# Eight heads in one pipeline: states and output of a head beside grams, inverse and attention of the next

## The reference, cut to what matters

```python
# A: sparse attention (the indexer's choice arrives as an additive mask)
logits = q @ k.T * 128 ** -0.5 - slope[h] * abs(t - s)      # masked
o_a = softmax(logits) @ v * silu(z_A)
# B: gated DeltaNet
qkv = silu(causal_conv(qkv_b, width 4));  q, k = l2norm(q), l2norm(k)
gc = cumsum(g);  decay = exp(gc[i] - gc[j]) where j <= i
M = I + strict_lower((beta * k) @ k.T * decay)
u, w = M^-1 @ (beta * v), M^-1 @ (beta * k * exp(gc))
for each chunk:                                   # here tiles of 128 tokens
    v_new = u - w @ S
    o = (q * exp(gc)) @ S + (q @ k.T * decay) @ v_new
    S = S * exp(gc_last) + (k * exp(gc_last - gc)).T @ v_new
o_b = rmsnorm(o) * silu(z_B)
y = x + concat(o_a, o_b) @ w_out;  final rmsnorm
```

## Time and profile before

| | us |
|---|---|
| three runs | 3327.34, 3342.03, 3343.69 |
| median | 3342.03 |
| span of the profiled execution | 3344.3 |

### The profile page before, as it was taken

One profiled execution on the slowest core, in us unless ns is written; L12 is line 12 of the kernel. 1 busy time (PEld: TensorE's weight loads), 2 busy tenths in 40 slices (PEclk: granted clock), 3 DMA queues, 4 the chain that ended last, 5 costly groups with the idle time before them and its releaser, 6 DMA issues. The chain is left out here.

```text
span 3344.3 us, 46103 instructions
## 1 busy us (share of the span) xinstructions
PE 2967.6 (89%) x16691; PEld 2657.3 (79%) x16691; DVE 1357.6 (41%) x2550; ACT 1025.5 (31%) x1995; POOL 887.9 (27%) x607
## 2 busy tenths in 40 slices
PE   4999899999999999999995588788878885799997
PEld 3999598998989899899995477667767774487876
DVE  6000101917463260705000667767776763214042
ACT  4111112213121211212112455565555553222221
POOL 6222021121212122121222223313422330155553
PEclk6999699999999999999997699999999997599998
DMA  3221222121212212122224111121121013346553
GB/s 129 62 65 60 43 69 73 49 72 49 67 57 64 62 60 73 56 66 63 69 64 133 36 49 50 41 69 34 35 69 48 27 41 88 125 155 208 175 180 120
DMA packets 271700, 255.47 MB, mean 76 GB/s; under 512 B 58712, under 2 KB 222752, under 8 KB 269152
## 3 DMA queue, kind: packets, MB, share of 16 engines
q1 hardware_dynamic: 261536, 208.80, 21.1%
q10 hardware_dynamic: 10048, 45.27, 3.3%
HBM read 190.48 MB, written 63.56 MB: 76 GB/s over the span
## 5 line engine op out<-in xcount | busy, mean ns | idle before, releaser
L394 PE MATMUL bank<-hH,wL 128*128 128x384 f32 (+1 forms) x2928 | 981.5, 335 | 14.9 <-POOL wL L311 14.9
L395 PE MATMUL bank<-hL,wH 128*128 128x384 f32 (+1 forms) x2928 | 980.1, 335 | 0.0
L396 PE MATMUL bank<-hH,wH 128*128 128x384 f32 (+1 forms) x2928 | 979.9, 335 | 0.0
L311 POOL TENSOR_TENSOR wL<-raw,wH 128x512 fp32r<-128x512 f32 x244 | 314.6, 1290 | 1388.7 <-ACT wH L328 1388.7
L394 PEld LDWEIGHTS bank<-hH,wL 128*128 128x128 f32 (+1 forms) x2928 | 550.1, 188 | 19.2 <-issue 18.5
L395 PEld LDWEIGHTS bank<-hL,wH 128*128 128x128 f32 (+1 forms) x2928 | 550.0, 188 | 0.8
L396 PEld LDWEIGHTS bank<-hH,wH 128*128 128x128 f32 (+1 forms) x2928 | 550.0, 188 | 0.7
L328 ACT ACTIVATE wH<-raw 128x512 fp32r<-128x512 f32 x244 | 154.2, 632 | 1019.3 <-PE bank L396 964.4
L1949 POOL TENSOR_TENSOR owL<-oraw,owH 128x2048 fp32r<-128x2048 f32 x48 | 225.5, 4700 | 271.4 <-ACT owH L1969 271.4
L506 DVE TENSOR_SCALAR score<-relued,w_idx 128x512 f32<-128x512 f32 (+3 forms) x10 | 7.8, 778 | 683.5 <-ACT relued L353 683.1
L1026 POOL TENSOR_TENSOR Bm<-A,keep_level 128x512 f32<-128x512 f32 x168 | 207.8, 1264 | 216.6 <-DVE A L1547 121.3
(11 more groups left out here) (297 smaller groups left out, 4028.8 us busy)
## 6 DMA issues: line engine op xcount, KB each, us to landing
raw<-in_w_in SPq DMA_DIRECT2D x240, 256.0 KB, 2.8
oraw<-in_w_out SPq DMA_DIRECT2D x48, 1024.0 KB, 5.0
proj_scratch<-ptbuf ACTq DMA_DIRECT2D x60, 576.0 KB, 2.8
xin<-proj_scratch SPq DMA_DIRECT2D x24, 512.0 KB, 4.8
mraw<-mix_scratch SPq DMA_DIRECT2D x12, 768.0 KB, 5.6
x<-in_x_prompt SPq DMA_DIRECT2D x8, 1024.0 KB, 5.0
out_y_prompt<-yv ACTq DMA_DIRECT2D x8, 1024.0 KB, 4.0
ox<-in_x_prompt SPq DMA_DIRECT2D x8, 768.0 KB, 6.6
```

The costliest lines, as they stand in the source:

```text
L311: pool.tensor_tensor(wL[c % 2][:, :, :], raw[c][:, :, :], wH[c % 2][:, :, :].bitcast(F32), ALU.subtract).then_inc(low_ready, 1)
L394: pe.matmul(o, low, hH[:, kk, tok], start=first, stop=False)
L395: pe.matmul(o, high, hL[:, kk, tok], start=False, stop=False)
L396: last = pe.matmul(o, high, hH[:, kk, tok], start=False, stop=end)
```

## The change

- All eight heads are written out; no loop is left in the stage. One list holds ten iterations, -2 to 7. Iteration i takes from head i the states (M), samples (S) and output (O), from head i+1 turns, grams, inverse and solves (D) and the attention (A), from head i+2 the convolution and its norms (N). Each step has a place between 0 and 1 in its iteration, and the list is sorted by it:

```diff
+def spread(first, last, steps):
+    return [(first + (last - first) * (i + 0.5) / len(steps), step) for i, step in enumerate(steps)]
+def iteration(i):
+    placed = []
+    if 0 <= i < H:
...
+        placed += spread(0.0, 0.36, states) + spread(0.36, 0.52, sample) + spread(0.52, 0.66, out)
...
+    if 0 <= i + 1 < H:
...
+        placed += spread(0.0, 0.07, turns) + spread(0.07, 0.26, grams) + spread(0.26, 0.30, first)
+        placed += spread(0.30, 0.93, levels) + spread(0.93, 1.0, solves)
...
+        placed += spread(0.0, 0.95, attend)
...
+    if 0 <= i + 2 < H:
...
+        placed += spread(0.05, 0.12, taps) + spread(0.12, 0.46, conv) + spread(0.46, 0.50, gates)
+        placed += spread(0.66, 0.90, natural) + spread(0.90, 1.0, norms)
...
+        placed += [(0.78, ("L_x", i + 3, 0))]
+    return [step for _, step in sorted(placed, key=lambda item: item[0])]
```

- PSUM: banks 0 and 1 serve states, samples, output and the turns of N in this order; banks 2 to 4 serve D; 5 and 6 the logits; 7 probabilities and values. The levels lag by one step, with two copies of WT, and both products of a step share a bank with its first one:

```diff
+        def w_bank(s):
+            return D_BANK + (0 if s == 0 else (2 * s - 1) % 3)
+        def z_bank(s):
+            return D_BANK + ((2 * s + 2) % 3 if s < NS - 1 else (2 * s + 1) % 3)
...
-                    if s >= LAG:
-                        r = s - LAG
+                    if s >= 1:
+                        r = s - 1
```

- Decays: mask and cumulated gates are summed in PSUM, for both triangles at once; ACT takes the exponential straight from there, the row's own gate as its bias. The grams are multiplied for two tiles at a time:

```diff
+                            pe.matmul(out, K["identb"][:, :], K["maskTN"][:, s, halves, :], start=True, stop=False)
+                            for part in range(2):
+                                last = pe.matmul(out, K["glog"][:, h, part, t:t + 1].to_broadcast([P, P]), K["cum2"][:, s, :, :], start=False, stop=part == 1)
...
+                        do(de[p % 2][:, t - lo, t_half, :], cum[:, t - lo, t_half, :], ACT.Exp, bias=K["gates"][:, h, G_NEG, t:t + 1])
+                        last = do(de[p % 2][:, t - lo, n_half, :], cum[:, t - lo, n_half, :], ACT.Exp, bias=K["gates"][:, h, G_POS, t:t + 1], scale=-1.0)
```

- Convolution: prompt and samples lie in one row per channel, the samples' old inputs between them as padding, so that a tap is one instruction over 1179 columns:

```diff
-                    V.scalar_tensor_tensor(out=y[:, n, 0:SEQ], in0=xin[:, n, j:j + SEQ], scalar=w, in1=y[:, n, 0:SEQ], op0=ALU.mult, op1=ALU.add).then_inc(convolved.sem, 1)
-                    ys = y[:, n, SEQ:].rearrange("p (b t) -> p b t", b=DEC_B)
-                    V.scalar_tensor_tensor(out=ys, in0=xsm[:, n, :, j:j + DEC_T], scalar=w, in1=ys, op0=ALU.mult, op1=ALU.add).then_inc(convolved.sem, 1)
+                    V.scalar_tensor_tensor(out=y[:, n, :], in0=xc[:, n, j:j + YC], scalar=K["cw"][:, n * H + h, 3 * DEC_B + j:3 * DEC_B + j + 1], in1=y[:, n, :], op0=ALU.mult, op1=ALU.add).then_inc(convolved.sem, 1)
```

- Attention: the distance term and the extreme value are one DVE instruction per part of at most 512 columns; the probabilities are scaled by their sum before they are turned, so that the product with v comes out turned, and the turn of the result is gone:

```diff
+                    V.tensor_tensor_reduce(out=lg[t % 2][:, c:e], in0=big[:, LG_BANK + i % 2, 0:e - c], in1=K["alibi"][:, at + c:at + e], scale=-SCALE, scalar=smallest,
+                                           op0=ALU.add, op1=ALU.min, accum_out=am[:, t, q // 4:q // 4 + 1]).then_inc(lg_ready.sem, 1)
...
+                    V.tensor_scalar(lg[t % 2][:, 0:w], lg[t % 2][:, 0:w], am[:, t, 3:4], None, ALU.mult).then_inc(p_scaled.sem, 1)
...
-                            last = pe.matmul(big[:, 7, 0:P], PT[t % 2][:, kb, :], K["vN"][:, kb, kv, :], start=(kb == 0), stop=(kb == t))
+                        last = pe.matmul(big[:, PV_BANK, 0:P], K["vN"][:, kb, h // GROUP, :], PT[t % 2][:, kb, :], start=(kb == 0), stop=(kb == t))
```

```diff
-                    if t >= 2:
+                    if t:
                         wait(pe, o_ready, h, t)
-                    pe.matmul(big[:, 2 + t % 2, 0:P], qkT[:, t, 0, :], S[:, :], start=True, stop=True)
+                    pe.matmul(big[:, 1, 0:P], qkT[:, q_slot(h), t, :], S[:, :], start=True, stop=True)
```

More of the change, by code:

```diff
@@ L710, in _ @@
                 dve.wait_ge(drained, NT)
[L711 to L761, removed]
-    s = LEVEL_STEPS.index((SAMPLE_LEVELS - 1, 4)) + LAG + 4
-    for step, every in (("D_solve_sample", 0), ("D_sample_state", 2), ("D_sample_turn", 3), ("D_sample_new", 1), ("D_sample_out", 2)):
-        s += every
-        levels.insert(levels.index(("D_level", s)), (step, 0))
-    order += levels
-    rest = ([] if last else [("N_done", 0)]) + score(4)
-    for t in range(4, NT):
-        rest += attend(t, t + 1 < NT)
-    rest += [("A_turn_o", NT - 1)]
-    if not last:
-        k = len(rest) * 3 // 4
-        rest = weave(rest[:k], NORMS[2:]) + rest[k:]
-    states = [("D_solve", 0)]
-    for t in range(NT):
-        states += [("D_read", t)] + ([("D_solve", t + 1)] if t + 1 < NT else []) + [("D_state", t), ("D_square", t - 1 if t else NT)]
-    return order + weave(states, rest) + [("D_square", NT - 1)]
@@ L793, in run_heads, with whole_order @@
+def whole_order():
+    order = [("L_x", 0, 0)]
+    for i in range(-2, H):
+        order += iteration(i)
+    return order
 def run_heads(nc, io, scratch, keep, ident):
@@ L1191, in _ @@
[L1191 to L1196 removed]
+                    wait(act, lg_ready, h, PARTS_TO[t])
@@ new lines, in values @@
+                def values(h, t):
+                    wait(pe, p_ready, h, PARTS_TO[t])
+                    for kb in range(t + 1):
+                        last = pe.matmul(big[:, PV_BANK, 0:P], K["vN"][:, kb, h // GROUP, :], PT[t % 2][:, kb, :], start=(kb == 0), stop=(kb == t))
+                    last.then_inc(pv_done.sem, 1)
+                run({"N_tails": tails, "N_turn": natural, "D_turn": qk_turn, "D_gram": gram, "D_first": first, "D_level": level, "D_solve": solve,
+                     "M_read": read, "M_state": state, "S_state": sample_state, "S_turn": sample_turn, "S_out": sample_out, "O_out": out,
+                     "A_logits": logits, "A_turn_p": turn_p, "A_values": values})
@@ L1540, in gram @@
[L1540 to L1547 removed]
+                    wait(dve, rooted, h, 1)
@@ L1629, in kept_tensors @@
+                run({"N_pads": pads, "N_conv": conv, "N_sum": sums, "N_norms": head_norms, "N_unit": unit, "D_gram": gram, "D_first": first, "D_level": level,
+                     "M_read": read, "M_state": state, "S_new": sample_new, "S_out": sample_out, "O_norm": out_norms, "O_out": out,
+                     "A_bias": bias, "A_norm": normalise, "A_gate": gate})
 def kept_tensors(nc, ctx):
```

1020 lines of the change are left out of this document (500 added, 520 removed).

## The result

The changed kernel takes 3302.91 us in the median of four runs (3300.03 to 3304.17), the kernel before 3342.86 beside it: ratio 0.9876, 95% interval 0.9851 to 0.9901. It is faster, by 40 us (1.2%); the forecast was 3212 us, 131 less. The direction held, the size did not: a third of the gain came.

A forecast was written before the change was run, and what follows sets the result against it. No engine was full, PE nearest; its 84.3 us of passes a head at 86% gave period P = 98. Ends and seven periods, 168 + 7P, replaced 986.6 us: T = 2525.7 + 7P = 3212 us, range 3135 to 3320.

The forecast's parts named there:

- P: Period of one head in the pipelined eight-head stage: 118.1 us before, forecast 98, with 92 to 104 as its range.
- Iteration -2: Start of the pipeline, the first head's convolution alone: 43 us (40 to 50) in place of 51.5.
- the tail: Last iteration, only the last head's states, samples and output: 38 us (30 to 48).
- the tables: Set-up ahead of the stage, 24 short transposes, two DMAs, small DVE steps: +2 us (0 to +5).
- 86%: Share of a full iteration that PE's 84.3 us of passes were taken to fill, giving a period of 98 us.
- The waits that I named: Norms to next head's first turn, SiLU block, inverse's first steps, state reading behind output sum: 2 to 4 us each, 14 in all.
- iteration 6 without convolution, P - 4: Second-last iteration, with no convolution left to do: 4 us shorter than a full one, 94 at P = 98.
- Iteration -1: Second iteration at the pipeline's start, without states: some 72 us of PE work, 88 us (75 to 105).
- Dense: Rival: three chains fill each other's gaps on PE as in the 96% stretch; P = 88, 3142 us; chance 0.15.
- One step of lag: Rival: PE waits 1.2 us for ACT's copy in each of 27 inverse steps; P = 126, 3408 us; chance 0.12.
- DVE held by POOL: Rival: port lock delays 20 DVE instructions 1.5 us each, DVE 98; P near 108, 3282 us; 0.20 with slower mixes.
- Nothing comes of it: Rival: waits of one order on in-order engines line heads up again; P 114 to 118, 3324 to 3352 us; chance 0.08.

## Why the prediction was wrong

**What held.** The range of 3135 to 3320 us holds the time, but not by the forecast's own mechanism: that ended at P = 104, and 112.65 falls under the 0.20 kept for "DVE held, and slower mixes up to P = 114". PE's work: 84.0 us priced, 84.3 forecast. DVE 70.2 a period (68), ACT 57.6 (59), POOL 32.1 (35.9), five table loads, PE's records 665 (a few under 675). Iteration -2 and the tail came 2 and 6 us under their terms; the tables cost 2.8 for 2. The loop's 3.0 us on issue are gone, but PE's first reading of a state stands 2.5 us on issue instead, because the state's clearing on DVE comes behind the two scalings of the norms.

**What failed** is one step: "I take 86%, midway between the 75% of the two large stages and 96%: 98 us." One density was put over three stages that have different limits. By stage, at 86%, the front would have taken 24.3 us, the levels 65.8, the end 7.6; they took 33.1, 67.3 and 12.2. So 8.8 and 4.6 of the 14.7 us lie in front and end, where the trace of before already had 51%, and where the change put two chains, but little of PE's other work: attention was spread by count of steps, and its first tiles are the small ones. In their place the runs show a front whose length hangs on the preparation of the next head, which stands in the same queues: 33.1 us as it is, 29.7 with most of the convolution's columns gone, 26.1 in iteration 6, which has none of that preparation. (The clock rises on the way, from 0.91 to 0.99 and 0.96, and no run parts its share.) The end is held by the norms: it takes 7.9 us with them moved ahead, though the levels pay that back. The run with four times the turns shows that PE's passes don't set the front's length there, the run with the largest tiles first that filling it pays.

**The waits that I named** were sized nearly right: first steps 4.2 us (3.07 and 1.14 in a row), SiLU block 2.3, reading for the output sum 2.3, norms 2.5, together 11.3 where 14 stood. They were not the whole: PE's gaps of over 0.15 us in the timeline sum to 18.6 us a period, and the remaining 10.0 (112.6 - 84.0 - 18.6) are passes that last longer than priced, alone or at 1.2 GHz. The granted clock of the three stages (0.91, 0.98, 0.81) makes 13 us of a period at the lower clock; at most half of that is lost. The prediction had no term for it in the period.

**A second mis-sized term**: iteration 6 without convolution, P - 4. It came out at 93.8 as forecast, but that is luck: P was 14.7 too small and the deduction 14.9, since the full iteration is 18.9 longer, not 4. Taking most of the columns from the multiply-adds gave 6.7 of that, clock included; the taps and SiLUs on ACT, the turns and the norms are the rest, which no run took apart. Iteration -1, with convolution and without states, took 99.0 where 88 stood: its front has some 15 us of passes in 28.9.

**The rivals.** *Dense* fell: only the levels came near. *One step of lag* fell: PE's second product waits 2.3 us a period for the copy, once, at the SiLU block, against 32 needed:

```profile
PE big L1280 <- ACT WT L1040: 2.3, 1, 2.3
```

*DVE held by POOL* would have given 108, near the result, by another way than what happened: the nine long convolution steps take 1645 ns in the mean of a period against a median of 1442, 1.8 us in all, and DVE is busy for 70.2 us, not 98:

```profile
L1399 DVE SCALAR_TENSOR_TENSOR y<-xc,keep_cw,y 128x1179 f32<-128x1179 f32 x9 | 14.8, 1645 | 0.0
```

The Trainium skill, SBUF — State Buffer, "Who interferes with whom", has the one that comes second block for the other's whole instruction; single steps here (1434 to 2298 ns) agree, their sum is just small. But POOL holds more than these: the two large first steps that stand beside its `Bm` (L1004) took 1.29 and 1.16 us, and the shortest of that form 0.79. With them DVE lost 2.8 us a period, 1.9 of it in the front, and no run took POOL away. *Nothing comes of it* (114 to 118) was nearest in its mechanism, the waits of one order on in-order engines; its lower end lies 1.3 us above the period measured.

**Left open.** The changed kernel, the one with early norms and the one with 27 more passes have the same period within 0.02 us, though PE stops in different places in them, and two kernels with the largest tiles first share 109.23. The settled periods 109.23, 112.64 and 116.05 lie 3.41 us apart, and the sums of two periods of the three kernels that alternate (221.9, 225.3 and 228.7) lie as far. What ties different orders to such steps was not found. Until it is, a change of 3.4 us a period here is one step, not the price of what was moved, and an unchanged period may hide a change that is smaller.

## What to carry to other kernels

Price the busiest engine's passes for each stretch of a pipeline and set them against the length of the chain that stands in that stretch: one density for the whole period hides the stretches in which no density can be had. In this order for in-order engines, work that was moved mostly came back as time in the stretch that took it, unless that stretch was waiting: six edits of places or banks gained nothing in the period, taking 8.7 us of DVE's busy time away gained 6.7 (with a higher clock), and giving the waiting stretch the engine's largest independent pieces gained 3.4 us a period.

## What was not expected of the hardware

Behind PE's waits the granted clock fell to 1.2 GHz within each iteration, in the middle of a period in which PE is busy for 83% of the time (93.3 of 112.6 us): the same products of values took 0.12 us a pass and, 8 us later, 0.22. Raising it in one stretch (0.74 to 0.87) did not shorten the period, so it followed the waits there and was not their cause. The Trainium skill, TensorE: Matmul & The Clock Gate, "Terms", takes the lost share of the time at the lower clock as the penalty; the share is half here, which makes an estimate of 6.6 of the 13 us of a period. The run with 27 more passes disagrees for its stretch: less of that time, the same period.
